# The layer norm of the conv branch: chunk sums on POOL, one factor per token spread by TensorE, its pieces set into the steps of the search

## The reference

```python
def layer_norm(x, g, b):
    mu = jnp.mean(xf, axis=-1, keepdims=True)
    var = jnp.mean(jnp.square(xf - mu), axis=-1, keepdims=True)
    y = (xf - mu) * lax.rsqrt(var + EPS)
    return y * g + b
...
def trunk_layer(x, conv_past, ffn_past, attend, p):
    xn = rms_norm(x, g_attn)
    a_in, q, k, v, qi, ki, wi, ga, gb = split_in(xn @ w_in)
    glu = a_in[..., :D_CONV] * jax.nn.sigmoid(a_in[..., D_CONV:])
    h = layer_norm(causal_dwconv(glu_ext, conv_w, conv_b), ln_g, ln_b)   # D_CONV = 512 channels
    y_a = jax.nn.silu(h) @ w_a_out
    o = attend(...)        # indexer scores, top 256 keys of each query, softmax over them
    x = x + (sigmoid(ga) * y_a + sigmoid(gb) * (o @ w_b_out)) @ w_o
    ...                    # then the gated ConvFFN
```

## Time and profile before

| | us |
|---|---|
| median of 3 runs | 1265.8 (1265.8, 1249.7, 1267.23) |
| span of the profiled execution | 1231.5 |
| PE busy | 1122.3 (91%) |
| DVE busy | 781.3 (63%) |
| ACT busy | 310.2 (25%) |
| POOL busy | 181.3 (15%) |

### The profile page before, as it was taken

How to read it: one execution, slowest core, us unless ns; L and a number is a source line. 1 busy time by engine, 2 the same in 40 slices (tenths; PEclk the granted TensorE clock), 3 DMA queues, 4 the chain that set the end, 5 groups by cost and what they waited for, 6 DMA issues and landing times. The chain is left out here.

```text
span 1231.5 us, 16971 instructions
## 1 busy us (share of the span) xinstructions
PE 1122.3 (91%) x6816; PEld 904.7 (73%) x6816; DVE 781.3 (63%) x1567; ACT 310.2 (25%) x633; POOL 181.3 (15%) x191
## 2 busy tenths in 40 slices
PE   5999799999789999978759799999999999989995
PEld 3668688664567733445435489999999999989995
DVE  5299999688799899877642163286666656622220
ACT  2111233222201234423213214223232212322120
POOL 0011110000011223155673200000000000001102
PEclk9999899999899999976878899999999999999998
DMA  9110550013243545255785522032323232223320
GB/s 306 45 68 7 179 182 1 18 51 137 69 169 122 162 156 174 75 162 157 226 269 176 158 90 60 1 93 79 99 74 103 70 103 69 72 76 91 113 80 28
DMA packets 109160, 134.51 MB, mean 109 GB/s; under 512 B 8085, under 2 KB 76077, under 8 KB 108036
## 3 DMA queue, kind: packets, MB, share of 16 engines
q1 hardware_dynamic: 90661, 76.52, 20.6%
q0 software_dynamic: 13344, 45.70, 11.9%
q10 hardware_dynamic: 5077, 11.20, 2.6%
HBM read 127.89 MB, written 5.51 MB: 108 GB/s over the span
## 5 line engine op out<-in xcount | busy, mean ns | idle before, releaser
L1253 PE MATMUL G<-xnH,whi 128*128 128x274 f32 x704 | 205.3, 292 | 1.4 <-DVE aext L1895 1.0
L1254 PE MATMUL G<-xnL,whi 128*128 128x274 f32 x704 | 203.5, 289 | 0.0
L1255 PE MATMUL G<-xnH,wlo 128*128 128x274 f32 x704 | 202.9, 288 | 0.0
L978 PE MATMUL G<-xnT,wring 128*128 128x280 f32 x512 | 137.8, 423 | 8.8 <-ACT sgb L1973 3.7
L1835 DVE TENSOR_TENSOR wlo<-wraw,whi 128x2048 fp32r<-128x2048 f32 (+1 forms) x38 | 76.4, 2011 | 92.2 <-ACT whi L2337 91.4
L1253 PEld LDWEIGHTS G<-xnH,whi 128*128 128x128 f32 x704 | 132.4, 188 | 1.8 <-issue 1.2
L1254 PEld LDWEIGHTS G<-xnL,whi 128*128 128x128 f32 x704 | 133.4, 189 | 0.1
L1255 PEld LDWEIGHTS G<-xnH,wlo 128*128 128x128 f32 x704 | 133.1, 189 | 0.0
L978 PEld LDWEIGHTS G<-xnT,wring 128*128 128x128 f32 x512 | 98.7, 199 | 38.3 <-issue 6.4
L2464 POOL DMA_INDIRECT ksel<-in_cache_k_dram,gather_row x64 | 72.7, 1136 | 336.7 <-DVE gather_row L1701 180.1
L1253 PE MATMUL G<-hfH,whi 128*128 128x274 f32 x352 | 103.2, 293 | 0.0
(11 more groups left out here) (408 smaller groups left out, 1999.5 us busy)
## 6 DMA issues: line engine op xcount, KB each, us to landing
wraw<-in_w_up_dram SPq DMA_DIRECT2D x44, 512.0 KB, 5.1
wring<-in_w_in_dram SPq DMA_DIRECT2D x8, 2048.0 KB, 7.8
wraw<-in_w_down_dram SPq DMA_DIRECT2D x16, 704.0 KB, 4.7
qB<-scr_q SPq DMA_DIRECT2D x32, 256.0 KB, 3.6
wring<-in_w_in_dram ACTq DMA_DIRECT2D x3, 2048.0 KB, 9.8
wring<-in_w_o_dram SPq DMA_DIRECT2D x2, 2048.0 KB, 8.2
toep<-scr_toep SPq DMA_DIRECT2D x1, 2432.0 KB, 15.7
wqi<-in_w_in_dram SPq DMA_DIRECT2D x2, 1024.0 KB, 9.5
```

Source lines behind the costliest of these rows:

```text
L978: last = pe.matmul(out[:, i, 0:b - a], w[:, j, c:c + P], x[:, j, a:b], start=(j == 0), stop=(j == depth - 1))
L1253: pe.matmul(out, w_hi, x_hi, start=start, stop=False)
L1254: pe.matmul(out, w_hi, x_lo, start=False, stop=False)
L1255: return pe.matmul(out, w_lo, x_hi, start=False, stop=stop)
```

## The change

The column sums: POOL adds the four chunks of `hT` (three adds of 128 x 560 into `lnsum`), and TensorE multiplies only this one by ones. The squares: POOL adds the chunks of `hsq` in the same way, and TensorE, in step 1 of the search, multiplies each tile of 128 tokens of the sum by one column of ones, so that a token's sum stands in one partition (128 x 5). VectorE makes the root there in step 2, ScalarE puts each factor on a diagonal in step 3, TensorE spreads them in step 4 (ones times the diagonals gives the factor in all partitions), VectorE multiplies `hT` in step 6, and ScalarE applies SiLU at step 8. `hsq` moves to the region of `gluT`. The results `("ln", 1)` and `("ln", 2)` stand behind `ga` 1 and `ga` 2 in `products`.

```diff
-    products += [("sc", b) for b in range(DEC_BATCH - 1)] + [("ln", 0), ("sc", DEC_BATCH - 1), ("ln", 1)]
+    products += [("sc", b) for b in range(DEC_BATCH - 1)] + [("ln", 0), ("sc", DEC_BATCH - 1)]
...
-    products += FILL
+    products += FILL[:2] + [("ln", 1), FILL[2], ("ln", 2)] + FILL[3:]
...
-        def norm_sums(stage):
...
-            src = (hT, hsq)[stage]
+        def norm_sums():
+
+            out = begin(("ln", 0))
+            pe.wait_ge(S["ln_sum"], 3)
             for i, (a, b) in enumerate(halves()):
-                for c in range(KC):
-                    last = pe.matmul(out[:, i, 0:b - a], ones, src[:, c, a:b], start=(c == 0), stop=(c == KC - 1))
+                last = pe.matmul(out[:, i, 0:b - a], ones, lnsum[0][:, a:b], start=True, stop=True)
+            last.then_inc(g_ready, 1)
+
+        def norm_square_sums():
+
+            out = begin(("ln", 1))
+            pe.wait_ge(S["ln_sum"], 6)
+            for r in range(NT):
+                t0, rows = tiles(r)
+                last = pe.matmul(out[0:rows, 0, r:r + 1], lnsum[0][:, t0:t0 + rows], ones[:, 0:1], start=True, stop=True)
+            last.then_inc(g_ready, 1)
+
+        def norm_spread():
+
+            out = begin(("ln", 2))
+            pe.wait_ge(S["ln_sq"], KC + 1)
+            for r in range(NT):
+                rows = ROWS[r]
+                last = pe.matmul(out[:, r // 4, r % 4 * P:r % 4 * P + rows], ones[0:rows, :], lndiag[0:rows, r, 0:rows], start=True, stop=True)
             last.then_inc(g_ready, 1)
...
-        norm_sums(1)
...
         for i in range(COMPARE + 1):
+            if i == 1:
+                norm_square_sums()
             fill(filled_by(i))
+            if i == 4:
+                norm_spread()
             pe.wait_ge(S["cnt_ready"], i + 1)
...
+        step(dve.memset(st(300, 24), 1.0))
...
-        def norm_take(stage):
...
-                step(dve.tensor_scalar(halved(lnt[:, 0, :]), src[:, :, 0:HALF], 1.0 / D_CONV, EPS, ALU.mult, ALU.add), free)
-                rsqrt(lnt[:, 1, :], lnt[:, 0, :], lnt[:, 2, :])
-                for c in range(KC):
-                    step(dve.tensor_tensor(hT[:, c, :], hT[:, c, :], lnt[:, 1, :], ALU.mult), S["ln_ready"])
...
+        def norm_rows():
...
+            v, y, a = st(300, NT), st(308, NT), st(316, NT)
+            step(dve.tensor_scalar(v[0:ROWS[-1], NT - 1:], src[0:ROWS[-1], 0, NT - 1:NT], 1.0 / D_CONV, EPS, ALU.mult, ALU.add))
+            step(dve.tensor_scalar(v[:, 0:NT - 1], src[:, 0, 0:NT - 1], 1.0 / D_CONV, EPS, ALU.mult, ALU.add), free)
+            rsqrt(y, v, a)
+            step(dve.tensor_copy(a, y), S["ln_ready"], free=True)
+
+        def norm_scaled():
...
+            x = src[:, :, :].rearrange("p a b -> p (a b)")[:, 0:T]
+            for c in range(KC):
+                step(dve.tensor_tensor(hT[:, c, :], hT[:, c, :], x, ALU.mult), S["ln_ready"], free=True)
+            step(dve.tensor_copy(stat[:, 262:263], src[:, 0, 0:1]), free, free=True)
...
-        norm_take(1)
...
                 prompt_score(i)
+            if i == 2:
+                norm_rows()
+            if i == 6:
+                norm_scaled()
             sample_take(i)
...
+        def norm_diagonals():
+
+            act.wait_ge(S["ln_ready"], KC + 1)
+            for r in range(NT):
+                rows = ROWS[r]
+                last = act.activation(lndiag[0:rows, r, 0:rows], ident[0:rows, 0:rows], ACT.Copy, scale=st(316 + r)[0:rows])
+            step(last, S["ln_sq"], free=True)
...
-        norm_silu()
         for i in range(COMPARE + 1):
+            if i == 3:
+                norm_diagonals()
+            if i == 8:
+                norm_silu()
...
+        def channel_sum(x):
+
+            for out, a, b in ((lnsum[0], x[:, 0, :], x[:, 1, :]), (lnsum[1], x[:, 2, :], x[:, 3, :])):
+                pool.tensor_tensor(out[:, :], a, b, ALU.add).then_inc(S["ln_sum"], 1)
+
+        conv_done(pool)
+        channel_sum(hT)
+        pool.wait_ge(S["ln_sum"], 2)
+        pool.tensor_tensor(lnsum[0][:, :], lnsum[0][:, :], lnsum[1][:, :], ALU.add).then_inc(S["ln_sum"], 1)
+        pool.wait_ge(S["ln_sq"], KC)
+        channel_sum(hsq)
+        pool.wait_ge(S["ln_sum"], 5)
+        pool.tensor_tensor(lnsum[0][:, :], lnsum[0][:, :], lnsum[1][:, :], ALU.add).then_inc(S["ln_sum"], 1)
```

More of the change, by code:

```diff
@@ L269, in build_in @@
     wkw = q("wkw", [P, KM, KW])
-    hsq = nc.alloc_sbuf_tensor_at("hsq", [P, KC, T], F32, offset=SEL)
-    lnt = nc.alloc_sbuf_tensor_at("lnt", [P, 3, T], F32, offset=QKT + KC * T * 4)
+    hsq = nc.alloc_sbuf_tensor_at("hsq", [P, KC, T], F32, offset=SGB)
+    lndiag = nc.alloc_sbuf_tensor_at("lndiag", [P, NT, P], F32, offset=QKT + KC * T * 4)
+    lnsum = [nc.alloc_sbuf_tensor_at(f"lnsum{i}", [P, T], F32, offset=M1 + (KM - 2 + i) * T * 4) for i in range(2)]
     decwin = nc.alloc_sbuf_tensor_at("decwin", [P, NS, CONV_W], F32, offset=SA)
@@ L474, in build_in @@
     names = """cols_ready cols_done toep_ready toep_done toep_scr toep_loaded x_sq x_scaled x_trans xn_done qk_nat
-        qk_sq nat_trans nat_done t1_ready t1_done w_diag q_stored ki_trans ki_done sc_ready sc_done newsc_ready
+        qk_sq nat_trans nat_done t1_ready t1_done w_diag q_stored ki_trans ki_done ln_sum sc_done newsc_ready
         seg_ready seg_done pi_ready pi_relu pi_acc cnt_ready bis_ready pi_tail
@@ L943, in _ @@
             if b == LN_SUM:
-                norm_sums(0)
+                norm_sums()
         pe.wait_ge(S["ki_done"], 2 * DEC_BATCH)
@@ L1466, in halved, with norm_center @@
             return x.rearrange("p (i t) -> p i t", i=2)
-        def norm_take(stage):
-            src, free = bank(("ln", stage))
-            ready(dve, ("ln", stage))
-            if stage == 0:
-                conv_done(dve)
-                for c in range(KC):
-                    step(dve.scalar_tensor_tensor(halved(hT[:, c, :]), src[:, :, 0:HALF], -1.0 / D_CONV, halved(hT[:, c, :]), ALU.mult, ALU.add), S["ln_ready"])
-                step(dve.tensor_copy(stat[:, 262:263], src[:, 1, HALF - 1:HALF]), free)
-            else:
-                dve.wait_ge(S["toep_scr"], 16)
-                step(dve.tensor_scalar(halved(lnt[:, 0, :]), src[:, :, 0:HALF], 1.0 / D_CONV, EPS, ALU.mult, ALU.add), free)
-                rsqrt(lnt[:, 1, :], lnt[:, 0, :], lnt[:, 2, :])
-                for c in range(KC):
-                    step(dve.tensor_tensor(hT[:, c, :], hT[:, c, :], lnt[:, 1, :], ALU.mult), S["ln_ready"])
+        def norm_center():
+            src, free = bank(("ln", 0))
+            ready(dve, ("ln", 0))
+            conv_done(dve)
+            for c in range(KC):
+                step(dve.scalar_tensor_tensor(halved(hT[:, c, :]), src[:, :, 0:HALF], -1.0 / D_CONV, halved(hT[:, c, :]), ALU.mult, ALU.add), S["ln_ready"], free=True)
+            step(dve.tensor_copy(stat[:, 262:263], src[:, 1, HALF - 1:HALF]), free, free=True)
+        def norm_rows():
+            src, free = bank(("ln", 1))
+            ready(dve, ("ln", 1))
+            v, y, a = st(300, NT), st(308, NT), st(316, NT)
[4 more added lines that the diff above has]
+        def norm_scaled():
+            src, free = bank(("ln", 2))
+            ready(dve, ("ln", 2))
+            x = src[:, :, :].rearrange("p a b -> p (a b)")[:, 0:T]
+            for c in range(KC):
+                step(dve.tensor_tensor(hT[:, c, :], hT[:, c, :], x, ALU.mult), S["ln_ready"], free=True)
+            step(dve.tensor_copy(stat[:, 262:263], src[:, 0, 0:1]), free, free=True)
         def branch_take(n):
@@ L1502, in _ @@
             if b == LN_SUM:
-                norm_take(0)
+                norm_center()
         dve.wait_ge(S["newsc_ready"], 1)
```

7 lines of the change are left out of this document (1 added, 6 removed).

## The result

| | us |
|---|---|
| kernel before, median of 20 runs | 1262.51 (1249.7 to 1267.23) |
| changed kernel, median of 20 runs | 1267.31 (1259.34 to 1273.49) |
| ratio | 1.0044 [1.0025, 1.0063], that is +5.5 us |
| profiled execution of the changed kernel | 1265.02, its span 1263.2 |

Forecast were +9.3 us and 1275. The changed kernel is slower, inside the range, by about 60% of what the sum said (the two medians alone differ by 4.8 us). Weighted by their intervals the three give 1.0045, **+5.6 us**. The three lie further apart than their intervals allow, so this mean is no better known than to about 2.5 us.

What follows compares the result with a forecast made beforehand. The prediction took TensorE to set the search's start and both engines to be nearly full inside it; its terms summed to +9.3 us (about +4 to +16) on a base of 1265.8, giving 1275 us, range 1252 to 1289.

Steps and rivals of the forecast that it cites:

- turn and last page's scores: Before the search: turn earlier without square sums, -1.0 us; last cache page's scores partly at half clock, +1.2 us.
- fills behind the second gap: TensorE's fills before the search: half clock after the gap ahead of the turn, +2.5 us (0.5 to 3.4).
- step 1: Search step 1: no table load before the gates, fill at full clock, -1.2 us (bounds -1.6 and +0.5).
- root, step 2: VectorE in search step 2: root of the factor per token, 2.8 us less a 0.52 wait, +2.3 us.
- spread, step 4: TensorE in search step 4: ten records of 128 columns spread the factors, +1.2 us (0.9 to 1.6).
- scaling, step 6: VectorE in search step 6: four products and a one-column copy, 3.3 us less 0.5, +2.8 us.
- half clock inside the search: TensorE idle about 2.5 and 3 us in steps 2 and 6; one slowed fill counted, +1.5 us (0 to 3).
- The first gap: TensorE waiting 2.0 us for POOL's column sums; half clock then delays the last cache page's scores, +1.2 us.
- part 1: Square sums leave the place before the turn of the scores, which then waits for the reduce alone, -1.0 us.
- POOL blocks VectorE: Rival: POOL's six adds, 7.2 us, slow VectorE beside them and push the last cache pages' reduces; 1282 us, chance 0.10.
- Absorbed: Rival: slack in the steps or a transfer late anyway hides the delay; +0 to +3 us, 1267, chance 0.17.
- Faster by a later half-clock stretch: Rival: new timing removes half-clock stretches at the search's end and in the attention behind; 1264 us, chance 0.12.

Runs made afterwards that it cites:

- e10_after_third: The changed kernel, unaltered, measured a third time; +9.8 us [6.8, 12.9] against the kernel before, ratio 1.008.
- e4_delay: Kernel before with seven more compares, results unused, on VectorE in step 2 of the search; +6.1 us [2.4, 9.7], ratio 1.0048.
- e6_no_factor: Changed kernel without square sums on TensorE, root, diagonals, spread and scaling; +2.7 us [0.1, 5.3] against the kernel before, ratio 1.0022.
- e2_warm: Changed kernel with filler products keeping TensorE busy in the two gaps before the search; -2.3 us [-5.7, 1.1] against the kernel before, ratio 0.9982.
- e8_pe_sums: Changed kernel with column sums made by TensorE from four chunks again, POOL adding only squares; +4.8 us [1.2, 8.4] against the kernel before, ratio 1.0039.
- e12_delay20: Kernel before with fifteen more compares, results unused, on VectorE in step 2 of the search; +22.6 us [19.4, 25.9], ratio 1.0184.
- e9_silu_warm: Kernel before with SiLU at step 8 and five filler products on TensorE at the search's end; -1.7 us [-4.5, 1.2], ratio 0.9986.
- e11_silu_again: Kernel before with only SiLU moved to step 8 of the search, second measurement; -4.9 us [-7.7, -2.2], ratio 0.996.
- e1_after_again: The changed kernel, unaltered, measured a second time; +1.3 us [-2.0, 4.5] against the kernel before, ratio 1.001.

## Why the prediction was right on the path and wrong on the clock

The path held: the search's start belongs to TensorE, VectorE's 11.8 us of norm were covered, taking them away freed nothing, and work put into the steps costs its length and reaches the end. The step that failed is the price of TensorE's clock (parts 3, 4 and 8): I took the half clock as following from each idle time of about 2 us, and full clock as following where an idle time goes away. The runs showed neither: 2.42 us of idle time had the half clock behind it in one profile of three, 2.25 and 2.24 us in none of five, and in step 1 the half clock stayed. The size so did not hold: +9.3 against +5.6. By the terms:

| term | forecast | first profile after | e10_after_third |
|---|---|---|---|
| turn and last page's scores | -1.0 + 1.2 | +0.8 | -1.8 |
| fills behind the second gap | +2.5 | +2.3 | +1.8 |
| step 1 | -1.2 | -0.1 | -0.1 |
| root, step 2 | +2.3 | +2.2 | +2.2 |
| spread, step 4 | +1.2 | +1.3 | +1.3 |
| scaling, step 6 | +2.8 | +2.2 | +2.2 |
| half clock inside the search | +1.5 | 0 | 0 |
| sum | +9.3 | +8.6 | +5.5 |

The first two terms are split at the start of the turn of the scores; the parts of the last columns add up to the table's interval within 0.2. That the first profile comes to 8.6, close to 9.3, is luck: there the errors (+0.6, -0.2, +1.1, -0.1, +0.1, -0.6, -1.5) cancel. And 1275 was 7.7 us too high, of which 3.3 are the base.

**Half clock inside the search** (part 8, "I count one") is the step that failed outright. Both gaps that I forecast at 2.5 and 3 us came, at 2.25 and 2.24, and the clock stayed at 1.00. I had reasoned from the gap of 1.7 us at 180, a short gap with the half clock behind it, to any gap as long. But the gaps of these kernels say that a gap's length doesn't decide alone: 2.42 us ahead of the last page's scores had the half clock behind it in one profile and not in two others, 2.25 in step 2 had it in none of the five profiles with these steps, 8.66 in e4_delay had.

**The first gap** (part 3, +1.2, bounds 0 and 2.2) is a draw between two values: at half clock the scores take 6.31 us, VectorE waits 2.51 us, and the turn comes 2.6 us later, above my bound; at full clock they take 3.68 and the gap costs nothing. One of three profiles of this kernel shows the slow draw. With the fast one the turn comes 1.8 us earlier than before instead of the 1.0 of part 1: 1.2 from the square sums, and 0.4 of the rest from the centring operations, which no longer wait for each other.

**Step 1** (part 4) had its three numbers right and its clock wrong. The gates start at once, TensorE resumes 0.66 us after instead of 2.08, the one-column products take 1.23 (forecast 1.2). But the fill stays at half clock, 3.84 us, where I took 2.1. The gap is shorter, and the fill behind the ten short products is as slow as behind the gap of the earlier trace rows: without the products, the two earlier gaps still open (e6_no_factor), step 1 is 3.0 us, and with the products and the two gaps filled (e2_warm) 4.2; the fill takes 2.15 us in both. So neither alone brought the half clock, by one profile each. This error of 1.1 us goes the other way and hid part of the first two.

**Scaling** (part 7) was costed from the earlier trace rows, 742 ns each with the distance between operations that wait for themselves, 3.3 us with the copy. The changed kernel marks the four `free=True`: they last 0.73 us each and start 0.65 us apart, 2.68 us in all and 2.75 with the copy; the term was 0.6 us too much.

The rivals. *POOL blocks VectorE* is excluded: the reduce beside POOL's add takes 1.99 us as elsewhere, and e8_pe_sums without three of the adds is no faster. The adds took 1.35 us, above the 1.2 forecast and under the 1.7 that the cover bore. The Trainium skill, "GPSIMD Engine Reference", Key points, confines the contention to VectorE instructions with two SBUF inputs or in a two-port mode; the rows beside these adds agree. The one small operation there with two SBUF inputs, `newsc<-spare,pack`, takes 0.46 us beside POOL's last add in e10_after_third and 0.18 in the kernel before; it holds nothing up. *Absorbed* is excluded for the search, where nothing of the three steps was hidden; behind it, e12_delay20 speaks against it, and a slope between 0.70 and 0.92 with a scatter of 3.1 us leaves room for a small part. *Faster by a later half-clock stretch* did not happen: VectorE's wait at the search's end is 3.7 us instead of 4.2 in the profiles after, and in e9_silu_warm, where that gap is filled, a stretch at half clock stands 33 us later.

The Trainium skill, "ScalarE: Activation LUTs", What ACT_TABLE_LOAD costs, would have a switch cost 2.66 us with its drain. In e11_silu_again SiLU's first operation starts 0.01 us behind the 1.28 us of the load. No drain shows here, and two loads at step 8 cost the search nothing.

What stays open: why the kernel without its factor was not faster, and why three measurements of one kernel spread over 8.5 us with intervals that don't meet. The search is not the reason. The draws of the half clock are the likely one. The runs' own clocks bear it out in part: against the kernel before on its chip e1_after_again lost 3.4 us less of full clock and e10_after_third 5.0 us more, which at 0.64 is 5.4 of the 8.5 us. What decides the draws is not shown.

## What to carry to other kernels

Ask first which engine starts the next stage; VectorE's 11.8 us of visible work were worth nothing there, while a table load of 1.28 us in front of one gate was worth 3. A loop whose engines are both full is a dear place for work: the same operations cost the search 6.9 us inside it and 3.3 ahead of it. Take the parts of a change apart before keeping or dropping it: only the late SiLU paid, -3.2 and -4.9 us.

## What the runs showed of the hardware

- One kernel, unaltered, had medians of 1261.0, 1228.9 and 1228.8 us on three chips. A span from one and a median from another must not be added.
- TensorE's clock after an idle time is not a function of that time alone: 2.42 us, then 0.54 (over 194 to 209) in one profile and 1.00 (over 193 to 198) in another, with the same code and the same operations before it. 2.25 us inside the search had 1.00 behind it in five profiles, 8.66 us had 0.54.
- Ten products of one column (1.23 us) between idle time and a fill left that fill at half clock, 3.84 us; with the two earlier gaps filled, the second up to 18 us ahead, it ran at full clock, 2.15 us, behind the same ten, and so it did with the gaps open and without the ten.
- VectorE operations of 128 x 560 that last 0.73 to 0.74 us start 0.78 us apart when each waits for itself and 0.65 us apart when it doesn't.
- A POOL add of 128 x 560 from SBUF took 1.35 us, three of them 4.1 us, and a VectorE reduce beside it was not slowed.
